# First layer's index queries and differential heads as seven block products each, with x read a second time

## What is computed

```python
h = rmsnorm(x, g_pre_mix[layer])                    # 512 x 1024
proj = jnp.einsum('bsd,dc->bsc', h, w_in[layer])
(q_a, k_a, v_a, q_i, k_i, w_i, q_d, k_d, v_d) = jnp.split(proj, SPLIT_POINTS, axis=-1)
q_i = apply_rope(q_i.reshape(B, S, IDX_HEADS, IDX_DIM), cos, sin)
...
# indexer: I[t,s] = sum_h w[t,h] relu(q_idx[t,h].k_idx[s]); each query keeps its top 128 keys
logits = jnp.einsum('bqhd,bsd->bqhs', qi, k_idx_f)
score = jnp.einsum('bqhs,bqh->bqs', jax.nn.relu(logits), wi) * idx_scale
_, sel = lax.top_k(score, topk)
...
# differential heads: queries and keys are roped too
p = probs(q1, k1f) - lam * probs(q2, k2f)
o = jnp.einsum('bhqs,bshe->bqhe', p, vf)
```

## Time and profile before

| | us |
|---|---|
| median of 3 runs | 1680.06 (1676.94 to 1681.64) |
| the profiled execution | 1683.46 |
| its span in the trace | 1681.6 |
| PE busy in the span | 1625.8 |
| DVE busy in the span | 752.8 |
| first plain group starts, stage three starts | 15.02, 144.34 |

### The profile page before, as it was taken

One profiled execution on the slowest core, in us unless ns is written; L12 is line 12 of the kernel. 1 busy time (PEld: TensorE's weight loads), 2 busy tenths in 40 slices (PEclk: granted clock), 3 DMA queues, 4 the chain that ended last, 5 costly groups with the idle time before them and its releaser, 6 DMA issues.

```text
span 1681.6 us, 18977 instructions
## 1 busy us (share of the span) xinstructions
PE 1625.8 (97%) x7334; PEld 1000.3 (59%) x7334; DVE 752.8 (45%) x1551; ACT 383.8 (23%) x821; POOL 261.3 (16%) x334
## 2 busy tenths in 40 slices
PE   7999999999999999999999999999999999998986
PEld 4444454578888888887876788644533333333332
DVE  3387786455453635456856355253512121111111
ACT  4443663510000000023245224101311111110111
POOL 1000000000000000007521225114022222221211
PEclk9999999999999999999999999999999999999998
DMA  5531113030222221324110112746899999999995
GB/s 189 125 76 50 51 51 138 14 113 0 101 70 80 101 100 61 105 67 182 57 60 36 50 51 65 228 165 254 339 362 416 417 419 418 420 414 418 422 416 221
DMA packets 76293, 307.87 MB, mean 183 GB/s; under 512 B 13165, under 2 KB 14322, under 8 KB 63276
## 3 DMA queue, kind: packets, MB, share of 16 engines
q1 hardware_dynamic: 65584, 291.60, 44.0%
q0 software_dynamic: 9872, 12.91, 3.7%
q10 hardware_dynamic: 748, 2.15, 0.3%
HBM read 309.09 MB, written 17.83 MB: 194 GB/s over the span
## 4 chain that ended last, share of the span: by engine, by line
PE 86%; DMA 8%; DVE 3%; ACT 2%; issue 1%; POOL 0%; POOLq 0%; SPq 0%; DVEq 0%; ACTq 0%
PE ps L1438 12%; PE ps L1309 12%; PE ps L1265 12%; PE ps L1725 11%; PE ps L1134 9%; DMA W<-in_w_expert_up 8%; PE ps L1742 6%; PE ps L1169 3%; PE ps L1130 3%; PE ps L1603 3%; PE ps L1629 3%; PE ps L1188 1%; PE ps L1719 1%; PE ps L1512 1%; PE ps L1086 1%; PE ps L1501 1%
## 5 line engine op out<-in xcount | busy, mean ns | idle before, releaser
L3116 DVE SCALAR_TENSOR_TENSOR smb<-smb,ptb,ps 64x512 f32<-64x512 f32 x34 | 38.3, 1125 | 277.9 <-ACT smb L2215 277.9
L1134 PE MATMUL ps<-W 128*128 128x512 f32 (+1 forms) x336 | 149.3, 596 | 1.6 <-ACT W L1862 1.6
L1725 PE MATMUL ps<-W,gb 128*64 128x512 f32 x480 | 131.1, 607 | 5.0 <-DMA W<-in_w_expert_up 5.0
L1725 PE MATMUL ps<-W,cmask 128*64 128x512 f32 x480 | 133.6, 609 | 2.3 <-DMA W<-in_w_expert_up 2.1
L1438 PE MATMUL ps<-W 128*128 128x256 f32 x576 | 128.7, 380 | 0.0
L1438 PEld LDWEIGHTS ps<-W 128*128 128x128 f32 x576 | 108.3, 190 | 17.6 <-issue 3.6
L1265 PE MATMUL ps<-yT,W 128*128 128x256 f32 x512 | 113.0, 379 | 0.0
L1742 PE MATMUL ps<-W,ptb 128*64 128x512 f32 x464 | 108.9, 612 | 3.3 <-DVE ptb L3122 3.3
L1309 PE MATMUL ps<-W,mix 128*128 128x256 f32 x496 | 108.5, 379 | 0.0
L1134 PEld LDWEIGHTS ps<-W 128*128 128x128 f32 (+1 forms) x336 | 61.2, 188 | 75.1 <-issue 72.9
L1265 PEld LDWEIGHTS ps<-yT,W 128*128 128x128 f32 x512 | 97.3, 190 | 13.2
(11 more groups left out here) (489 smaller groups left out, 2542.0 us busy)
## 6 DMA issues: line engine op xcount, KB each, us to landing
W<-in_w_expert_up SPq DMA_DIRECT2D x25, 2048.0 KB, 38.0
W<-in_w_expert_down SPq DMA_DIRECT2D x24, 2048.0 KB, 26.5
W<-in_w_expert_gate SPq DMA_DIRECT2D x22, 2048.0 KB, 32.5
W<-in_w_in SPq DMA_DIRECT2D x16, 2048.0 KB, 7.6
W<-in_w_up SPq DMA_DIRECT2D x8, 2048.0 KB, 7.9
W<-in_w_down SPq DMA_DIRECT2D x8, 2048.0 KB, 7.8
W<-in_w_out SPq DMA_DIRECT2D x4, 2048.0 KB, 7.9
W<-in_w_expert_gate SPq DMA_DIRECT2D x8, 1024.0 KB, 34.4
```

Source lines behind the costliest of these rows:

```text
L1134: ins = pe.matmul(ps[0:n, bank, :], wv[:, k, j * P:j * P + n], hT[:, k, :], start=(k == 0), stop=(k == KT - 1))
L1725: ins = pe.matmul(ps[64 * part:64 * part + 64, 2, :], xsT[s][:, k, :], w[part][:, k, :], start=(k == 0), stop=(k == KT - 1))
L3116: dve.scalar_tensor_tensor(out=hid.rearrange("r (k p) -> r p k", k=4), in0=sgate.rearrange("r (p k) -> r p k", k=4), scalar=weight, in1=ps ...
```

## The change

Each of the four 512-column parts is now computed by `side_product(n)`, n from 0 to 27, seven products per part, in the order P1, P2, P5, P6, P3, P7, P4. Parts 0, 1, 2, 3 are QI, QD, KD, VD. What comes with it:

- POOL makes four weight sums per part (`fore_w_sums`, 4 pieces of 128x256 each), the first two as soon as the sixth product of the part before has run. Its transfers of `g_post_mix` and of the bias line now stand between these sums.
- DVE makes four sums of `hT` once (`fore_t_sum`, 128x1024 each). They are written over x, so x is loaded a second time, behind chunk 5.
- ACT keeps products P1 and P5 in SBUF (`fore_keep`). DVE adds the blocks with `fore_post`: seven operations of 128x512 per part, five of which read one operand from PSUM and two both from SBUF. It does so for the values too.
- The roped parts are turned only after that, so ACT's swaps read SBUF and start behind DVE's last addition of the half (`fore_rope` gives the count waited for), and two heads are turned one after the other (`FORE_ROPE`).
- Of the 48 top-k steps, 34 now stand before stage three: two behind each product from 14 to 21, three behind each from 22 to 27.
- The index key's group and the head weights come after part 0. The index scores stand behind products 10, 12, 14, 16, 18 and 20.
- The first chunk is loaded as two halves of 256 columns; PE computes P1 of part 0 on token tiles 0 and 1 before it turns tiles 2 and 3.

```diff
+        FORE_ROPE = {4: (0, 1), 6: (2, 3), 11: (5, 6), 13: (7, 8), 18: (9, 10), 20: (11, 12)}
+        IDX_AFTER = {10: 0, 12: 1, 14: 2, 16: 3, 18: 4, 20: 5}
...
+            first = ring_view(0, KT, 512)
+            sp.dma_start(first[:, :, 0:256], chunks[0][:, :, 0:256]).then_inc(first_cols_load, 16)
+            sp.dma_start(first[:, :, 256:512], chunks[0][:, :, 256:512]).then_inc(ring_load[0], 16)
+            load(1, chunks[1])
...
             for c in range(2, C_UP):
                 load(c, chunks[c])
+                if c == 5:
+                    for i in range(NT):
+                        sp.dma_start(x[:, i, :], io["x"][0, i * P:(i + 1) * P, :]).then_inc(x_load[i], 16)
...
+            pe.wait_ge(turn_evac, 4)
+            side_product(0)
             turn(T_PRE, [2, 3])
+            side_product(1)
             pe.wait_ge(turn_evac, 8)
...
+            for n in range(2, 7):
+                side_product(n)
+            dense1(0, (0, 1))
...
+            side_product(7)
+            side_product(8)
...
+            for n in range(9, 28):
+                side_product(n)
+                if n in IDX_AFTER:
+                    idx_scores(IDX_AFTER[n])
...
             pe.wait_ge(rope_done, 13)
-            pe.wait_ge(val_done, 4)
+            pe.wait_ge(side_read, 28)
...
+            def fore_swap(r):
+                src, done = fore_rope(r)
+                act.wait_ge(side_read, done)
+                if r >= 2:
+                    act.wait_ge(rope_done, r - 1)
+                for q in range(4):
+                    ins = act.activation(yT[32 * q:32 * q + 32, 4 + r % 2, :], src[32 * (q ^ 1):32 * (q ^ 1) + 32, :], ACT.Copy)
+                ins.then_inc(swap_done, 1)
...
+            for n in range(9, 28):
+                fore_post(n)
+                if n - 1 in IDX_AFTER:
+                    idx_sums(IDX_AFTER[n - 1])
+                for r in FORE_ROPE.get(n, ()):
+                    turn_pairs(r, fore_rope(r)[0], fore_rope(r)[0])
+                if n >= 14:
+                    for _ in range(2 if n < 22 else 3):
                         next(steps_left, None)
```

More of the change, by code:

```diff
@@ L466, in build @@
         ASIDE = -1
[L467 to L473, removed]
+        G1 = [("ki", 1, 0, kiT), ("wi", ASIDE, 0, None)]
         BESIDE1 = len(G1)
@@ L605, in side_bank @@
             return 4 + n % 2 if n < 35 else 5 if n < 49 else 4 + (n - 49) % 4
-        X_KEPT = [48 if i == 1 else 32 for i in range(NT)]
+        X_AGAIN = [48 if i == 1 else 32 for i in range(NT)]
+        X_KEPT = [n + 16 for n in X_AGAIN]
         CONV_BANK = (2, 3, 2, 3, 2, 1, 2, 1)
@@ L899, in side_h_sum @@
                 pool.tensor_tensor(side_h[n], a, b, ALU.subtract).then_inc(t_sums, 1)
[L900 to L905, removed]
+                pool.wait_ge(t_sums, FORE_T + 37 + n)
             def side_w_sums(c, part):
@@ new lines, in idx_scores @@
+            def idx_scores(p):
+                pe.wait_ge(rope_done, 5)
+                pe.wait_ge(ki_dup, 1)
+                for q, (i, h) in idx_part(p):
+                    group(q % 4, relu_done, q + 1)
+                    r = 64 * (h % 2)
+                    pe.matmul(ps[:, q % 4, 0:(i + 1) * P], qiT[r:r + 64, h // 2, i * P:(i + 1) * P],
+                              kiT[r:r + 64, 0:(i + 1) * P], start=True, stop=True).then_inc(idx_done, 1)
+            pe.wait_ge(turn_evac, 4)
+            side_product(0)
@@ L1869, in dense1 @@
                 bank = bank1(g)
-                swaps = count1(g, ("rope", "ki")) - 1
-                if kind in ("rope", "ki"):
+                swaps = rope_no(g)
+                if kind == "rope":
                     act.wait_ge(proj_done, g + 1)
-                    if swaps >= 2:
-                        act.wait_ge(rope_done, swaps - 1)
-                    if kind == "ki":
-                        act.activation(wi_rows, ps[64:72, bank, :], ACT.Copy)
-                    for r in range(4 if kind == "rope" else 2):
+                    act.wait_ge(rope_done, swaps - 1)
+                    for r in range(4):
                         ins = act.activation(yT[32 * r:32 * r + 32, 4 + swaps % 2, :],
@@ L1880, in dense1 @@
                     ins.then_inc(swap_done, 1)
-                    if kind == "ki":
-                        act.wait_ge(rope_done, swaps + 1)
-                        act.activation(kiT[64:128, :], kiT[0:64, :], ACT.Copy).then_inc(ki_dup, 1)
                 elif kind == "val":
@@ L2109, in gate_sigmoids @@
                 half, br_ = c // 2, c % 2
[L2110 removed]
+                act.wait_ge(side_read, FORE + 35 + 7 * c + (7 if upper else 4))
                 for j in ((2, 3) if upper else (0, 1)):
```

430 lines of the change are left out of this document (290 added, 140 removed).

## The result

The changed kernel takes 1705.78 us (median of 4 runs, 1704.47 to 1711.74) against 1678.50 for the kernel before on the same chip: ratio 1.0167, interval 1.0137 to 1.0198, 27.3 us slower. The forecast was 1702, in a range of 1686 to 1712. Each ratio is against the kernel before, run on the same chip beside the kernel in question.

What follows compares the result with a forecast made beforehand. DVE was taken to bound stage two: from 61.6, 86.3 of work, 13.1 of waits and 9 for POOL end at 170, PE's second stage-three scores come 22.3 later, and 1680.1 + 22 = 1702 us, range 1686 to 1712.

Steps and rivals of the forecast that it cites:

- DVE is the bound of stage two: Stage two: DVE's queue, not PE's, sets the end, by 17 us before any wait.
- The bare work, 86.3 us: DVE's work behind product 10: 65.2 old, 2.0 for a turn, 13.2 for additions, 5.9 for four more top-k steps.
- the waits, 13.1: DVE's idle time behind product 10: 3.1 for product 11, 11.6 for ACT's swaps, less 1.6 covered by index sums.
- POOL beside DVE, 9: Behind product 10, POOL's ten sums lengthen 18 DVE operations with both operands in SBUF by 0.5 each: 9 us.
- The end of product 10, 61.6: PE's walk through stage two ends product 10 at 61.6, where DVE takes over; no earlier wait was found.
- The clock, "up to 3": Start of stage three: PE's granted clock may fall after its pause, adding up to 3 us.
- PE alone would gain 13: PE's own queue before stage three would be 13 us shorter through the block products.
- PE's waits in front of the index scores: Stage two: PE waits for ACT and DVE (its two relu buffers), making the next additions late; no separate size.
- the worst rival: 14 us for POOL, 3 for the clock, PE's waits in front of the index scores: +32, 1712 and beyond; chance 0.05.
- The rival "PE decides, faster": Stage two: DVE's work PE needs is early, so PE sets the time: -13, 1667; chance 0.11.

Runs made afterwards that it cites:

- kernel with later steps: Changed kernel with 16 top-k steps before stage three in place of 34, the other 32 inside stage three: 1690.46 us, ratio 1.0070 to the kernel before.
- Taking the sums away: Changed kernel without POOL's weight sums of parts 1 to 3, semaphore counts kept: 1699.38 us, ratio 1.0120 to the kernel before.
- kernel with all parts turned first: Changed kernel, all four parts as products, with all of x turned ahead of the first block product: 1702.82 us, ratio 1.0141 to the kernel before.
- few steps: Changed kernel with 45 of the 48 top-k strike-out steps left out: 1681.60 us; kernel before with the same left out: 1678.40 us.
- two-part kernel, turned first: Changed kernel with only QI and QD as products, 30 top-k steps before stage three, all of x turned first: 1676.18 us, ratio 0.9980 to the kernel before.
- few steps and no turns: Changed kernel without 45 of 48 top-k strike-out steps and without swaps and turns of parts 1 and 2: 1671.36 us, ratio 0.9946 to the kernel before.
- kernel with the values: Changed kernel with QI, QD and VD as products, KD plain, all of x turned first: 1686.66 us, ratio 1.0049 to the kernel before.

## Why the prediction was right, step by step

- **DVE is the bound of stage two: right.** The kernel with later steps shows it (15.3 us back), and so does the row of 15.44 us in front of stage three.
- **The bare work, 86.3 us, and the waits, 13.1: right.** DVE ran from 64.77 to its first score at 172.86, 108.1 us. The forecast had 61.6 to 170, 108.4. The waits in between are 3.25 for product 11 and 9.5 for swaps, 12.7 in all. Less these and the 8.8 of the next point, 86.6 are left for the bare work.
- **POOL beside DVE, 9: right.** Taking the sums away cut DVE's busy time by 8.8. It gave back 7.4 at stage three and 6.4 in the end, since 1.1 turned into longer waits for swaps. The count behind the 9 was two too high: eight of POOL's sums, not ten, run behind product 10, but they took 29.9 us where 28 were put in, since they are slowed too.
- **The end of product 10, 61.6: 3.0 too early.** It ended at 64.6. The first product took 5.41 in place of 3.45, and the fourth waited 1.29 for its bank, which DVE frees only after its four sums of hT and the copies of the vectors (L2484). I had looked for waits on data and weight sums only, not for the bank. The kernel with all parts turned first puts a price on this stretch: 3.9 at stage three.
- **The clock, "up to 3", kept for the range only: it came.** The half group behind PE's wait took 6.10 in place of 3.70. DVE began its queue 3.0 late, and the last addition freed PE at 168.3, not 166. The forecast had PE's half group end 0.6 before DVE was through with the first scores. In the trace the half group ended last, at 175.1, and set the second scores. 2.3 later freed, 2.4 for the half group and 0.3 for the scores in front of it, less the 0.6, are the 4.4 us by which the second scores missed the forecast (26.7 against 22.3). So the time came out 27.3 us above the kernel before where 22 was forecast, and 4.4 of the 5.3 are here: the likeliest value left out the clock and the late start, and the range had room for them.
- **PE alone would gain 13: too much.** 8.8 were measured. The start ate some 4 of it: in that kernel the first product took 6.62, the bank was waited for as well, and the index key's group began at 43.68, where the forecast's walk has 39.7. The price of PE alone did not enter the forecast, since DVE decided.
- **PE's waits in front of the index scores** stood only in the worst rival. They came (10.4 us in four waits: 8.8 released by ACT, 1.6 by DVE). They did no harm in the sum, since PE still waited 15.44 us for DVE behind them, but with few steps they and the slow products behind them ate all of PE's gain.
- **The rival "PE decides, faster"** put its limit at 69 us of DVE's work behind product 10. In the changed kernel DVE needed 108.1. The two-part kernel, turned first, comes nearest to that rival: DVE's queue there ends 1.4 us behind the start of stage three, and it is the one that is faster.

## What to carry to other kernels

Seven products for eight save TensorE about an eighth of its time on them (24.2 us in place of 27.5 per part, by the rows) and hand VectorE seven additions. Count these against VectorE's idle time in the very stretch where they fall, with everything that it takes in order behind them, and convert only as many parts as fit: here two of four. A result that another engine must rearrange after the addition costs a hand-over there and back, and moving the consumer by one product only moved the wait. And the first matmuls after a pause are not a way to use the pause, if they stand in front of work that could run then.

## What the runs showed of the hardware

- A short pause of PE can be followed by slow matmuls. In the changed kernel, after a wait of 1.63 us and two index scores, the next product took 5.41 (3.62 elsewhere), and the mean granted clock from 84.9 to 90 was 0.67, part of the time at the lower of the two levels (1.2 and 2.4 GHz). After 15.44 us it was 0.59 from 169 to 175. It need not be: after 1.29 us in front of the fourth product, that product took 3.69. In the two-part kernel with the turning first the clock was 1.00 in every stretch looked at.
- The first product ahead of the second half of the turning took 3.72 to 6.62 us in eight traces with the same instructions there. First with the steps later, then with few steps and no turns:

```profile
13.22 3.72 PE L1216 MATMUL ps<-W 128*128 128x256 f32 x16 [1.95 <-DVE W L2420]
```

```profile
13.21 6.62 PE L1216 MATMUL ps<-W 128*128 128x256 f32 x16 [1.95 <-DVE W L2423]
```

- At the start the granted clock and the durations do not always agree. In the changed kernel the first product took 5.41 at a clock of 0.66 (13 to 18). In the kernel with few steps and no turns it took 6.62, and the clock row says 1.00 for the same stretch (13.3 to 19.8). Why is open.
- Contention slows both sides. DVE's turn operations, with both operands in SBUF, go from 0.69 to 1.21, and a sum of POOL's from 2.78 to 4.46. The Trainium skill, SBUF — State Buffer, section "Who interferes with whom", names this pair of instructions as the one that contends, by an exclusive lock. The trace agrees as to which operations are hit: in the kernel with the values the addition at 77.57, with one operand in PSUM, takes 0.67 right behind the slow turns, while POOL's sum runs on to 78.2.
